# Expert matmuls of a mixture-of-experts layer as three fp32r products of split operands

## The reference

```python
h = rmsnorm(x, g_norm_mix[l]) * (1.0 + sc_a) + sh_a
x = x + g_a * hybrid_mixer(h, ...)
h = rmsnorm(x, g_norm_moe[l]) * (1.0 + sc_m) + sh_m
x = x + g_m * grouped_moe(h, w_router, router_bias, w_exp_gate[l], w_exp_up[l], w_exp_down[l])

# in grouped_moe: xs are the tokens of an expert, in blocks
a = jax.nn.silu(jnp.einsum('nrd,ndf->nrf', xs, w_gate[blk_e])) * jnp.einsum('nrd,ndf->nrf', xs, w_up[blk_e])
y = jnp.einsum('nrf,nfd->nrd', a, w_down[blk_e]).reshape(-1, D) * slot_w[:, None]
out = jnp.zeros((N + 1, D), hf.dtype).at[slot_tok].add(y)[:N]
```

## Time and profile before

| | |
|---|---|
| time, median of 3 runs | 2341.64 us (2336.65 to 2341.66) |
| span of the profiled execution | 2337.3 us |
| PE busy in it | 2067.4 us, 88% |
| DVE, ACT, POOL busy | 29%, 23%, 10% |
| HBM read, written | 195.41 MB, 25.19 MB |

### The profile page before, as it was taken

One profiled execution on the slowest core, in us unless ns is written; L12 is line 12 of the kernel. 1 busy time (PEld: TensorE's weight loads), 2 busy tenths in 40 slices (PEclk: granted clock), 3 DMA queues, 4 the chain that ended last, 5 costly groups with the idle time before them and its releaser, 6 DMA issues.

```text
span 2337.3 us, 21396 instructions
## 1 busy us (share of the span) xinstructions
PE 2067.4 (88%) x7857; PEld 1277.0 (55%) x7858; DVE 669.5 (29%) x1325; ACT 532.7 (23%) x1140; POOL 230.4 (10%) x276
## 2 busy tenths in 40 slices
PE   6699999977888989889799999989739999999992
PEld 1354648366656767676667777745414444444440
DVE  2321210155444545464622222112311111111115
ACT  1221100034433424344511111101102121111112
POOL 1221210000100101111100000000030000000002
PEclk9799995957877869797899999999869999999996
DMA  7101311600000000000111121152304666465675
GB/s 282 56 18 36 67 42 50 228 12 1 1 1 1 1 1 1 1 1 1 37 36 36 36 68 41 36 216 72 108 18 162 251 234 230 182 240 199 229 266 224
DMA packets 116897, 217.52 MB, mean 93 GB/s; under 512 B 6616, under 2 KB 45616, under 8 KB 116688
## 3 DMA queue, kind: packets, MB, share of 16 engines
q1 hardware_dynamic: 105440, 181.12, 22.5%
q0 software_dynamic: 7920, 22.72, 2.7%
q10 hardware_dynamic: 3456, 12.58, 1.3%
HBM read 195.41 MB, written 25.19 MB: 94 GB/s over the span
## 4 chain that ended last, share of the span: by engine, by line
PE 81%; DVE 9%; issue 3%; ACT 3%; DMA 2%; POOL 1%; SPq 0%; DVEq 0%; ACTq 0%; POOLq 0%
PE psum L1668 14%; PE psum L1596 11%; PE psum L1402 8%; PE psum L1499 8%; PE psum L1684 7%; PE psum L1560 6%; PE psum L1621 5%; PE psum L1601 5%; PE psum L1528 4%; PE psum L1342 3%; PE psum L1418 2%; PE psum L1433 2%; PE psum L1456 1%; DVE negm L1120 1%; DVE arena L1168 1%
## 5 line engine op out<-in xcount | busy, mean ns | idle before, releaser
L1668 PE MATMUL psum<-arena,kv 128*128 128x512 f32 x768 | 335.2, 594 | 1.7 <-ACT kv L873 1.7
L1560 PE MATMUL psum<-kv,arena 128*128 128x64 f32 x1464 | 227.4, 307 | 63.4 <-DVE arena L1104 36.3
L1560 PEld LDWEIGHTS psum<-kv,arena 128*128 128x128 f32 x1464 | 220.3, 229 | 71.4 <-issue 38.3
L1668 PEld LDWEIGHTS psum<-arena,kv 128*128 128x128 f32 x768 | 146.5, 191 | 186.2 <-issue 186.2
L1596 PE MATMUL psum<-arena_r,kv_r 128*128 128x512 f32 x768 | 238.3, 391 | 0.0
L1499 PE MATMUL psum<-kv,heads 112*128 112x512 f32 (+7 forms) x384 | 192.1, 614 | 9.9 <-DVE arena L1128 9.1
L1402 PE MATMUL psum<-arena 128*128 128x512 f32 (+2 forms) x512 | 189.5, 524 | 1.6 <-DVE arena L939 1.6
L1596 PE MATMUL psum<-arena_r 128*128 128x512 f32 x384 | 169.7, 442 | 9.5 <-DVE arena_r L432 9.5
L1684 PE MATMUL psum<-arena,bc 128*128 128x512 f32 x384 | 171.2, 599 | 6.0 <-ACT bc L886 6.0
L1528 PE MATMUL psum<-ident,arena 128*128 128x128 f32 x828 | 157.8, 320 | 15.2 <-ACT arena L367 8.6
L1596 PEld LDWEIGHTS psum<-arena_r,kv_r 128*128 128x128 f32 x768 | 144.9, 189 | 41.0 <-issue 11.2
(11 more groups left out here) (318 smaller groups left out, 2119.3 us busy)
## 6 DMA issues: line engine op xcount, KB each, us to landing
arena<-in_w_exp_gate_dram SPq DMA_DIRECT2D x16, 2048.0 KB, 10.6
arena<-in_w_exp_up_dram SPq DMA_DIRECT2D x16, 2048.0 KB, 15.5
arena<-in_w_exp_down_dram SPq DMA_DIRECT2D x16, 2048.0 KB, 20.1
arena<-in_w_ada_dram SPq DMA_DIRECT2D x12, 2048.0 KB, 9.3
arena<-in_w_in_dram SPq DMA_DIRECT2D x24, 512.0 KB, 5.1
y_dram<-bc ACTq DMA_DIRECT2D x24, 512.0 KB, 8.0
arena<-in_w_in_dram SPq DMA_DIRECT2D x3, 2048.0 KB, 9.9
arena<-in_x_dram SPq DMA_DIRECT2D x8, 512.0 KB, 8.9
```

The source lines that it names most:

```text
L1560: mm = pe.matmul(psum[:, bank, c * HD:(c + 1) * HD], pt[:, j * P:(j + 1) * P], v, start=(j == 0), stop=(j == u["nb"] - 1))
L1668: mm = pe.matmul(psum[:, i, :], xsT[:, k, :], slot(3 * q + i)[:, k, :], start=(k == 0), stop=(k == NK - 1))
```

## The change

Four things change.

- The experts' gate, up and down matmuls become three fp32r matmuls each (`split_matmuls`, and the same written out for down). ACT copies each expert's weights to a high part (`expert_weights_hi`, 6 pieces of 128x2048, into one set of buffers `ew_hi` that every expert uses), DVE subtracts to get the low part, in place of the raw weights (`expert_weights_lo`). The tokens and the activation are split in the same way as they leave PSUM.
- The loop over blocks is written out expert by expert; the output of block j is copied and stored at the head of iteration j+1.
- `x1` also goes to DRAM (`x1_dram`) tile by tile and is read back into `res` after the last block, since `heads` now holds high parts.
- The second norm's scale and shift are spread over rows once (16 small matmuls, `mod_rows`) and put on `xn2` before it is stored, so the evacuations behind the transposes are plain copies or splits.

```diff
-            load_expert(0, 0, (0, 1))
+            load_expert(0, 0)
+            load_expert(0, 1)
             sp.wait_ge(dest_ok, 1)
...
+            for e in range(2, NE):
+                b_next = sp.value_load(plan_i[0:1, NE + e - 1:NE + e], min_val=1, max_val=N_BLK - 1)
+                for i, read in enumerate((gate_full, up_full, y_full)):
+                    sp.wait_ge(read, b_next + 1)
+                    sp.nop().then_inc(sp_go, 1)
+                    load_expert(e, i)
...
+            for n in range(NT):
+                sp.dma_start(res[n], x1_dram[n * P:(n + 1) * P, :]).then_inc(res_in[n], 16)
...
+            def expert_weights_hi(e, b_e):
+                for i, read in enumerate((gate_full, up_full, y_full)):
+                    act.wait_ge(expert_w[3 * (e % 2) + i], e // 2 * 16 + 16)
+                    if b_e is not None:
+                        act.wait_ge(read, b_e + 1)
+                    for c in range(2):
+                        cs = slice(c * SLOT // 2, (c + 1) * SLOT // 2)
+                        act.activation(ew_hi[i][:, cs], w_raw(e, i)[:, cs], ACT.Copy).then_inc(w_hi_ok, 1)
...
+            act.wait_ge(x1_out, 16 * NT)
+            expert_weights_hi(0, None)
...
+            for e in range(NE):
+                b_e, b_next = b_next, act.value_load(plan_i[0:1, NE + e + 1:NE + e + 2], min_val=1, max_val=N_BLK - 1)
+                if e:
+                    expert_weights_hi(e, b_e)
+                with act.Fori(b_e, b_next) as j:
+                    expert_out_act(j)
+                    act.wait_ge(gate_full, j + 2)
+                    act.activation(silu_g, psum[:, 0, :], ACT.Silu).then_inc(silu_ok, 1)
...
-                    dve.tensor_scalar(xn2, x1[:, n, :], stp[:, 1:2], None, ALU.mult).then_inc(xn2_ok, 1)
+                    else:
+                        dve.wait_ge(mod_rows_act, 1)
+                    own(dve.scalar_tensor_tensor(xn2, x1[:, n, :], stp[:, 1:2], a2_bc, ALU.mult, ALU.mult))
+                    dve.tensor_tensor(xn2, xn2, b2_bc, ALU.add).then_inc(xn2_ok, 1)
...
+            def expert_weights_lo(e):
+                for c in range(6):
+                    i, cs = c // 2, slice(c % 2 * SLOT // 2, (c % 2 + 1) * SLOT // 2)
+                    dve.wait_ge(w_hi_ok, 6 * e + c + 1)
+                    dve.tensor_tensor(ew_lo(e, i)[:, cs], w_raw(e, i)[:, cs], ew_hi[i][:, cs].bitcast(F32),
+                                      ALU.subtract).then_inc(w_lo_ok, 1)
...
+                with pe.Fori(b_e, b_next) as j:
+                    pe.wait_ge(xs_lo_ok, j + 1)
+                    pe.wait_ge(a_ok, j * 2 + 1)
+                    for i, full in enumerate((gate_full, up_full)):
+                        pe.wait_ge(w_lo_ok, 6 * e + 2 * i + 2)
+                        split_matmuls(psum[:, i, :], xs_hi, xs_lo, lambda k: hi[i][:, k, :], lambda k: lo[i][:, k, :],
+                                      NK).then_inc(full, 1)
+                    pe.wait_ge(xs_in, j * 16 + 32)
+                    expert_tokens(0, xsT_half)
+                    for c in range(2):
+                        pe.wait_ge(a_ok, j * 2 + 2 + c)
+                        for k in range(2):
+                            ins = pe.transpose(psum[:, (4, 7)[c], k * P:(k + 1) * P],
+                                               act_a[:, (2 * c + k) * P:(2 * c + k + 1) * P], ident[:, :])
+                        ins.then_inc(aT_full, 1)
+                    expert_tokens(1, xsT_full)
+                    pe.wait_ge(y_act, j + 1)
+                    pe.wait_ge(y_dve, j + 1)
+                    pe.wait_ge(w_lo_ok, 6 * e + 6)
+                    for k in range(4):
+                        if k % 2 == 0:
+                            pe.wait_ge(aT_hi_ok, j * 2 + k // 2 + 1)
                         for h in range(2):
+                            hs = slice(h * BANK, (h + 1) * BANK)
+                            pe.matmul(psum[:, 5 + h, :], aT_hi[:, k, :], lo[2][:, k, hs], start=(k == 0), stop=False)
+                            pe.matmul(psum[:, 5 + h, :], aT_hi[:, k, :], hi[2][:, k, hs], start=False, stop=False)
+                    pe.wait_ge(aT_lo_ok, j + 1)
+                    for k in range(4):
+                        for h in range(2):
+                            mm = pe.matmul(psum[:, 5 + h, :], aT_lo[:, k, :], hi[2][:, k, h * BANK:(h + 1) * BANK],
+                                           start=False, stop=(k == 3))
+                    mm.then_inc(y_full, 1)
```

More of the change, by code:

```diff
@@ L234, in hybrid_trunk @@
         probT = [tmp[:, (2 + i) * T:(3 + i) * T] for i in range(2)]
[L235 to L239, removed]
+        zs, zc, zl, cum = (part_of(1, i * T, (i + 1) * T) for i in range(4))
+        att = part_of(2)
+        prob_b, cmp_s, cmp_p = att[:, 0:T], att[:, 1024:1536], att[:, 1536:2048]
+        swa_s = [att[:, 2048 + i * 256:2304 + i * 256] for i in range(2)]
+        part, o_tok = att[:, 2560:3072], att[:, 3072:4096]
         negm = sb("negm", [P, 4])
@@ L469, in hybrid_trunk @@
[L469 to L477 removed]
+        xs = kv[:, 2 * D:3 * D]
@@ L484, in hybrid_trunk @@
+        pair_in, res_in = [sem(f"pair_in{n}") for n in range(NT)], [sem(f"res_in{n}") for n in range(NT)]
         scaled, comb_ok, out_st = sem("scaled"), sem("comb_ok"), sem("out_st")
@@ L523, in _, with load_expert @@
                 load(i)
[L525 to L528, removed]
+            def load_expert(e, i):
+                w = (wge, wue, wde)[i]
+                sp.dma_start(as_k(w_raw(e, i), i), w[e]).then_inc(expert_w[3 * (e % 2) + i], 16)
             wait_used(sp, L_OUT - 1)
-            load_expert(1, 1)
-            load_expert(0, 0, (2,))
+            for i in range(3):
+                load_expert(1, i)
+            load_expert(0, 2)
             sp.wait_ge(mix_done, 3 * 2 * NK)
@@ L854, in _ @@
             act.wait_ge(mix_done, 3 * 2 * NK)
+            act.wait_ge(y_ok, 4 * NK)
+            act.wait_ge(mod_rows, 1)
+            act.activation(a2_bc.rearrange("p (a d) -> p a d", a=2), psum[:, 4:6, :], ACT.Copy).then_inc(mod_rows_act, 1)
             for n in range(NT + 1):
@@ L1196, in _ @@
                     sums += 1
+            dve.wait_ge(y_ok, 4 * NK)
+            dve.wait_ge(mod_rows, 1)
+            own(dve.tensor_copy(b2_bc.rearrange("p (a d) -> p a d", a=2), psum[:, 6:8, :]))
             for n in range(NT + 1):
@@ L1611, in _ @@
             pe.wait_ge(y_ok, 4 * NK)
+            for i, m in enumerate((mod_a2, mod_b2)):
+                for k in range(NK):
+                    mm = pe.matmul(psum[:, 4 + 2 * i + k // 4, (k % 4) * P:(k % 4 + 1) * P], m[:, k:k + 1].to_broadcast([P, P]),
+                                   ident[:, :], start=True, stop=True)
+            mm.then_inc(mod_rows, 1)
             for h in range(2):
@@ L1649, in expert_tokens, with split_matmuls @@
                 ins.then_inc(full, 1)
+            def split_matmuls(out, lhs_hi, lhs_lo, rhs_hi, rhs_lo, n):
+                for k in range(n):
+                    pe.matmul(out, lhs_hi[:, k, :], rhs_lo(k), start=(k == 0), stop=False)
+                    pe.matmul(out, lhs_lo[:, k, :], rhs_hi(k), start=False, stop=False)
+                    mm = pe.matmul(out, lhs_hi[:, k, :], rhs_hi(k), start=False, stop=(k == n - 1))
+                return mm
             pe.nop().then_inc(xsT_full, 1)
+            pe.nop().then_inc(gate_full, 1)
+            pe.nop().then_inc(up_full, 1)
+            pe.nop().then_inc(y_full, 1)
             pe.wait_ge(xs_in, 16)
```

223 lines of the change are left out of this document (113 added, 110 removed).

## The result

The changed kernel takes 2282.97 us (median of 4 runs, 2279.34 to 2286.88) against 2341.65 us of the kernel before in the same session (4 runs, 2336.65 to 2343.57): a ratio of 0.9756 with an interval of 0.974 to 0.9772, 59 us faster. The profiled execution has a span of 2280.9 us, 56.4 less than before.

What follows compares the result with a forecast made beforehand. The prediction held that PE alone bounds the experts' stage (97% busy, full clock). Stage -39.5, start +1.3 and end +3 gave -35 us: span 2337.3 to 2302, median 2306, range 2270 to 2336.

Steps and rivals of the forecast that it cites:

- the likeliest case: Whole kernel: the forecast of 2306 us, with its own range of 2290 to 2320; chance 0.50.
- (a): Experts' stage: the clock holds across the gap at a change of expert; stage -68, time 2278 us; chance 0.22.
- The blocks: Experts' stage: 18.6 us a block without a change of expert (9), 21.2 with one (15) before the clock's loss.
- I take 2.2 (bounds 2.0 and 2.6): Experts' block: PE's time between up and down, for transposes and waits, 2.2 us against 2.36 before.
- The clock: At each change of expert: a 2.5 us gap drops the clock to 1.2 GHz for 4 us, losing 1.9 us.
- The start: Ahead of the experts: second norm's exposed part with the first token split, +1.3 us, bounds 0 and 2.4.
- the one on expert 0: Before the first gate: expert 0's six high and low pieces, 11.4 and 13.7 us, hidden beside routing and first gather.
- "0 to 2 us" for the spare stores: Before the routing table is read: spare stores to y_dram now come there, costing 0 to 2 us.
- The end: Combination: eight x1 loads start with the last store and gather, +3 us, bounds 0 and 6.
- (b): Change of expert: ACT and DVE pay 0 to 2 us each for register read and new code; 2336 us; chance 0.15.
- (c): Change of expert: the clock stays low far longer than 4 us; 14 us would give 2377 us; chance 0.06.
- (d): Experts' stage: weight loads bind, only above 32 us an expert; at 35, 2352 us; chance 0.03.

Runs made afterwards that it cites:

- e1: The changed kernel, but PE waits for the gate and up weights' low parts half by half, not both halves at once: 2270.87 us, ratio 0.9706.
- e4: The changed kernel, but x1 is read back into expert 14's freed gate and up slots while expert 15 runs: 2275.04 us, ratio 0.9731.
- e2: The changed kernel with the spare stores to y_dram moved behind the loads of expert 3: 2280.82 us, ratio 0.9743.
- e3: The changed kernel, but DVE begins expert 0's six subtractions only when all 16 routing-table scatters have landed: 2284.36 us, ratio 0.9763.
- e8: The changed kernel with the edits of both e2 and e3: 2277.72 us, ratio 0.9734.
- e7: The changed kernel with two needless DVE passes of 128x2048 ahead of each later expert's subtractions: 2351.92 us, one run.
- e9: The changed kernel with e4, e8, half-by-half waits for down too, reordered DVE work at the start and in each expert's first block: 2228.73 us, ratio 0.9524.
- e5: The changed kernel with one needless DVE pass of 128x2048 ahead of each later expert's subtractions: 2318.72 us, one run.

## Why the prediction was right, and where it was off

The forecast was 2306 us and faster; 2282.97 is faster and inside the range of 2270 to 2336, but outside the likeliest case's own 2290 to 2320. It lies nearest to rival (a), 2278, and the miss of 23 us is made of errors of both signs: the stage gave 34.9 more than forecast, the start cost 9.9 and the end 3.8 more, and the median lies 2.1 above the span and not 4.3.

**The blocks: right, a little dear.** A block without a change was put at 18.6 and took 18.10. Gate and up (10.9) and down (5.45) came out at 10.89 and 5.53; the term that was off is what lies between, "I take 2.2 (bounds 2.0 and 2.6)": it took 1.68, under the lower bound. A change was put at 21.2 and took 20.46: besides the same 0.5, the gap was 2.1 and not 2.5, since PE reached gate 7.80 us after the start of down and not 8.1. Over 9 and 15 blocks that is 4.5 + 11.1 = 15.6 us.

**The clock: the step that failed.** "So I expect a fall to 1.2 GHz at each change of expert" came true at 5 of 15. The same gap of 2.11 us stands before the gate at 1928.46 and at 1987.52; the windows (as in rows 1) of the four us behind the first, and one by one, from the first to the last that is not at 1.00 and one more (the row between is at 0.50 too), behind the second:

```profile
1928.00:1932.00 4.00, 3.54 (x16) 2.97 (x17) 4.00 (x3) 4.00 (x3) 0.57 (x1) 1.00 0.97 378
1988.00:1989.00 1.00, 1.00 (x4) 0.81 (x4) 1.00 (x1) 1.00 (x2) 0.00 (x0) 0.68 0.88 348
1989.00:1990.00 1.00, 1.00 (x4) 0.73 (x3) 1.00 (x2) 1.00 (x2) 0.56 (x1) 0.50 1.01 414
...
1991.00:1992.00 1.00, 1.00 (x4) 0.78 (x4) 1.00 (x2) 1.00 (x2) 0.00 (x0) 0.62 0.98 393
1992.00:1993.00 1.00, 1.00 (x6) 0.83 (x5) 1.00 (x1) 0.33 (x1) 0.00 (x0) 1.00 0.84 332
```

The length and price of a fall were near: about 3.4 us, costing some 1.6, against 4 and 1.9. But 5 falls are 8 us and not 28.5. The prediction made a rule out of a single gap of 1.69 us in the attention; the runs show that such a gap brings a fall sometimes, and the more often the longer it is. The Trainium skill's rule, TensorE: Matmul & The Clock Gate, section HAM oscillation, lets the clock fall only behind a longer gap. Its sum was nearer to the time than mine, but as a rule it doesn't hold here either: five gaps of 2.1 us brought a fall, and two of e1's gaps, of 1.76 and 1.74 us, did so too. What makes the one 2.1 us gap fall and the other hold stays open. It is not the work at that change, since e4, with the same work there, falls at other changes.

Together: 9 x 18.10 + 15 x 20.46 + 5 x 1.6 = 477.8, and the first block ran its first 4.8 us at half, 2.3 more: 480.1, against 481.0 measured and 513.9 forecast. The stage gave 2.0 more still because in the kernel before it measures 555.4 where the prediction had 553.4.

**The start: mis-sized, 1.3 put for 11.2.** The 1.3 was for the second norm with the first token split. They came out near it, at 1.0 for the norm and 0.6 from the table to the first gate; the other 1.1 us of the first scatter's delay lie ahead of the last tile and can't be put down to the change. The wrong step is the one on expert 0: "Expert 0's six high and low pieces (11.4 and 13.7 us) lie beside the routing and the first gather". They do lie beside it, but not free of charge: they stretch POOL's scatters by 6.5 us. "0 to 2 us" for the spare stores was near as the kernel stands: 2.0 against the kernel before, 2.4 against e2. Without DVE's delay they cost far more: 47.6 us from first scatter to first gate in e3, 37.2 in e8.

**The end: mis-sized, 3 put for 6.8.** The bounds of 0 and 6 were drawn from a store landing behind weights, 8.0 us in the median. Here it landed in 9.15 beside the loads of `x1` (e4 shows them to be the cause), 6.5 longer than the 2.66 of before.

**The rivals.** (a), the clock holds: 10 times of 15, and its total is nearest, partly by luck: its stage gained 68 of the 74.4 measured, and its two ends cost 4.3 where 18.0 were measured. (b), a price of leaving one loop and entering the next on ACT and DVE: not seen at the change shown: ACT's first copy (1921.87) starts with no idle time behind its token split, DVE's first subtraction starts 1.00 us behind its own and waits for ACT's piece, and a change costs less than its passes had been put at. (c), the clock stays low for long: the falls in the changed kernel last 3.4 us; in e7, with gaps of 5.8, 13 of the 15 last 6.8. (d), the loads bind: PE never waits for a weight, and ACT waits for one once, 2.0 us. The terms of the sum, measured and in brackets as forecast: stage -74.4 (forecast -39.5), start +11.2 (+1.3), end +6.8 (+3).

## What to carry to other kernels

A product that is split into cheap matmuls moves work to the engines that split. Look at the order in which they take their pieces and at what stands behind the pieces in their lists, then let the matmul start on each piece as it comes. e1 does only the last and finds the next lateness behind the first; e9 does both and takes out all 15 gaps, and the clock's falls with them. Before work is called hidden "beside" another engine's, ask what the two share: here the DVE passes and the spare stores lay beside the routing, and either would have held it up alone. When two causes cover each other, as in e2 and e3, undo both at once before judging either.

## What the runs showed of the hardware

- POOL's indirect DMA issues take 0.96 us alone and 1.86 to 2.87 us while DVE does a subtraction of 128x2048 float32 with both operands in SBUF; the first gather 3.0 instead of 0.99 (e3, e8). The Trainium skill, GPSIMD Engine Reference, section Specifications, says that POOL shares its SBUF interfaces with DVE and that instructions of DVE with two SBUF inputs contend; the trace agrees and gives the price.
- Behind a PE gap in a stretch that is otherwise dense with matmuls the clock fell at 24 of 75 changes (gap 2.1 us, five runs), 13 of 15 (3.4, e5) and 15 of 15 (5.8, e7); behind gaps of 1.7 to 1.8 us before the activation's transposes at 2 of 13 (e1). Which of the 2.1 us gaps brought it down differed from run to run.
- A 512 KB store issued 0.95 us after the first of eight loads of the same size landed in 9.15 us in place of 2.66; with the loads earlier (e4) its gather came 4.45 us after the output copy in place of 10.98.
